# Attention scores without the mask products: maximum and exponential over the seen columns only, in four pieces of 64 rows

## The reference

```python
# 16 heads, q and k of 128 + 64 features, 256 tokens, CHUNK = 64, Q_BLOCK = 128
q_chunk = (bi * Q_BLOCK + arange(Q_BLOCK)) // CHUNK      # bi = 0, 1
key_chunk = arange(256) // CHUNK
mask = key_chunk[None, :] <= q_chunk[:, None]            # a chunk sees itself and those before it
sc = einsum('bqhd,bkhd->bhqk', qb, k) * 192 ** -0.5
p = softmax(where(mask, sc, -inf))
out = einsum('bhqk,bkhd->bqhd', p, v)
```

## Time and profile before

| | |
|---|---|
| median of 3 runs | 1943.89 us (1943.64 to 1944.12) |
| the profiled execution, its own time | 1943.84 us |
| its span in the trace | 1942.4 us |
| PE busy | 1936.6 us, 100% of the span |
| PE weight loads (PEld) | 1649.1 us, 85% |
| DVE busy | 1336.7 us, 69% |
| ACT busy | 1000.7 us, 52% |
| latent attention's heads (first scores to last gate) | about 174 to 284 us |

### The profile page before, as it was taken

One profiled execution on the slowest core, in us unless ns is written; L12 is line 12 of the kernel. 1 busy time (PEld: TensorE's weight loads), 2 busy tenths in 40 slices (PEclk: granted clock), 3 DMA queues, 4 the chain that ended last, 5 costly groups with the idle time before them and its releaser, 6 DMA issues.

```text
span 1942.4 us, 25506 instructions
## 1 busy us (share of the span) xinstructions
PE 1936.6 (100%) x10030; PEld 1649.1 (85%) x10030; DVE 1336.7 (69%) x1963; ACT 1000.7 (52%) x1433; POOL 0.2 (0%) x4
## 2 busy tenths in 40 slices
PE   9999999999999999999999999999999999999999
PEld 7889988988888888898888888888888888888887
DVE  6756778887545557898688877589666444666654
ACT  5645555675556544575565655444444334444442
POOL 0000000000000000000000000000000000000000
PEclk9999999999999999999999999999999999999999
DMA  8555325455553455545534345555555555555562
GB/s 328 176 193 174 131 90 192 174 199 187 191 189 133 174 192 195 182 177 207 211 116 149 128 152 195 196 194 177 191 195 200 197 201 192 190 189 194 185 228 109
DMA packets 51707, 353.23 MB, mean 182 GB/s; under 512 B 5652, under 2 KB 7196, under 8 KB 9860
## 3 DMA queue, kind: packets, MB, share of 16 engines
q1 hardware_dynamic: 50016, 348.84, 50.2%
q10 hardware_dynamic: 1572, 2.75, 0.4%
HBM read 349.47 MB, written 2.11 MB: 181 GB/s over the span
## 4 chain that ended last, share of the span: by engine, by line
PE 93%; DVE 5%; ACT 1%; issue 1%; DMA 0%; ACTq 0%; DVEq 0%
PE bank L1197 92%; DVE WL L2121 2%; DVE AR L2298 0%; ACT WH L1624 0%; DVE ft L2882 0%; DVE AR L2411 0%; DVE XP L2294 0%; DVE AR L2408 0%; DVE XP L2396 0%; PE bank L1342 0%; DMA X<-in_x 0%; DVE AR L2287 0%; PE bank L1427 0%; DVE AR L2322 0%; DVE AR L2321 0%
## 5 line engine op out<-in xcount | busy, mean ns | idle before, releaser
L1624 ACT ACTIVATE WH<-raw 128x1024 fp32r<-128x1024 f32 x649 | 683.4, 1057 | 645.1 <-PE bank L1197 639.0
L2121 DVE TENSOR_TENSOR WL<-raw,WH 128x1024 fp32r<-128x1024 f32 x649 | 784.0, 1221 | 316.4 <-ACT WH L1624 313.1
L1197 PE MATMUL bank<-XP,WH 128*128 128x512 f32 (+2 forms) x1584 | 498.6, 389 | 0.6 <-DVE WL L2117 0.3
L1197 PE MATMUL bank<-WH,FP 128*128 128x512 f32 x1408 | 434.7, 389 | 0.1
L1197 PEld LDWEIGHTS bank<-XP,WL 128*128 128x128 f32 x1504 | 281.8, 187 | 59.4 <-issue 0.7
L1197 PEld LDWEIGHTS bank<-WH,FP 128*128 128x128 f32 x1408 | 264.3, 188 | 56.1 <-DVE WL L2121 1.0
L1197 PE MATMUL bank<-XP,WL 128*128 128x256 f32 (+1 forms) x1504 | 308.5, 279 | 0.1
L1197 PE MATMUL bank<-WH,XP 128*128 128x512 f32 (+1 forms) x960 | 301.2, 389 | 0.3 <-DVE WL L2121 0.3
L1197 PE MATMUL bank<-WL,FP 128*128 128x512 f32 x704 | 273.9, 389 | 0.0
L1197 PEld LDWEIGHTS bank<-XP,WH 128*128 128x128 f32 (+1 forms) x1584 | 248.1, 187 | 7.5 <-issue 1.4
L1197 PE MATMUL bank<-WH,AP 128*128 128x512 f32 x704 | 217.2, 389 | 0.0
(11 more groups left out here) (336 smaller groups left out, 1616.9 us busy)
## 6 DMA issues: line engine op xcount, KB each, us to landing
raw<-in_W SPq DMA_DIRECT2D x326, 1024.0 KB, 4.8
out<-XT ACTq DMA_DIRECT2D x8, 256.0 KB, 2.0
raw<-in_W SPq DMA_DIRECT2D x3, 512.0 KB, 6.7
X<-in_x SPq DMA_DIRECT2D x3, 512.0 KB, 12.6
AR<-rv SPq DMA_DIRECT2D x1, 1024.0 KB, 5.9
cst<-in_cst SPq DMA_DIRECT2D x1, 899.5 KB, 11.7
raw<-in_W SPq DMA_DIRECT2D x2, 256.0 KB, 4.3
AR<-in_sgu SPq DMA_DIRECT2D x1, 512.0 KB, 5.7
```

The lines of the kernel that those rows point to most:

```text
L1197: return pe.matmul(o, lhsT, rhs, start=start, stop=stop)
L1624: ac.activation(w_slot(WH, s), raw_half(hf), ACT.Copy).then_inc(s_hi, 1)
L2121: tt(w_slot(WL, s), raw_half(pl.half_of[s]), w_slot(WH, s).bitcast(F32), ALU.subtract).then_inc(s_lo, 1)
```

## The change

The two mask products of each head go, and `uv` with them. `max` and `exp` no longer run over all rows at once, one instruction for each query block, but in four pieces of 64 rows, each over the columns that these rows see: 64, 128, 192 and 256 columns. The columns that rows 0 to 63 don't see are set to zero once, in all four buffers `Pm`, ahead of the section; `exp` never writes them, and `norm`, `turn` and `pv` run over them as before. The constants `u` and `v` become unused room.

```diff
-        uv = sb("uv", 256, BF, at=a0_ + 4 * 15616)
+        SEEN = [(j, slice(64 * r, 64 * r + 64), slice(128 * j, (128, 384)[j] - 64 + 64 * r))
+                for j in range(2) for r in range(2)]
...
                     for j in range(2):
-                        mm(S[:, 0:128], a[j][:, 0:128], k[j][:, 0:128], j == 0, False)
-                    mm(S[:, 0:128], uv[:, 0:128], uv[:, 128:256], False, True)
+                        mm(S[:, 0:128], a[j][:, 0:128], k[j][:, 0:128], j == 0, j == 1)
                     for j in range(2):
-                        mm(S[:, 128:384], a[j][:, 128:256], k[j], j == 0, False)
-                    mm(S[:, 256:384], uv[:, 0:128], uv[:, 128:256], False, True).then_inc(s_msc, 1)
+                        ins = mm(S[:, 128:384], a[j][:, 128:256], k[j], j == 0, j == 1)
+                    ins.then_inc(s_msc, 1)
...
-                    ac.activation(p[:, 0:128], S[:, 0:128], ACT.Exp, scale=sc, bias=m[:, 0:1], accum_out=s[:, 0:1])
-                    ac.activation(p[:, 128:384], S[:, 128:384], ACT.Exp, scale=sc, bias=m[:, 1:2],
-                                  accum_out=s[:, 1:2]).then_inc(s_mex, 1)
+                    for j, rows, cols in SEEN:
+                        ins = ac.activation(p[rows, cols], S[rows, cols], ACT.Exp, scale=sc, bias=m[rows, j:j + 1],
+                                            accum_out=s[rows, j:j + 1])
+                    ins.then_inc(s_mex, 1)
...
-                    dv.tensor_copy(uv[:, 0:128], C("u"))
-                    dv.tensor_copy(uv[:, 128:256], C("v")).then_inc(s_krm, 1)
+                    for p in Pm:
+                        for o in (64, 320):
+                            ins = dv.memset(p[0:64, o:o + 64], 0.0)
+                    ins.then_inc(s_krm, 1)
...
-                    dv.tensor_reduce(m[:, 0:1], S[:, 0:128], AX, ALU.max)
-                    chain(dv.tensor_reduce(m[:, 1:2], S[:, 128:384], AX, ALU.max))
+                    for j, rows, cols in SEEN:
+                        ins = dv.tensor_reduce(m[rows, j:j + 1], S[rows, cols], AX, ALU.max)
+                    chain(ins)
                     ts(m, m, -sc, None, ALU.mult).then_inc(s_mmx, 1)
```

More of the change, by code:

```diff
@@ L142 @@
 for _name, _w in [("ident", 128), ("bones", 128), ("U", 128), ("mC", 256), ("mS", 384), ("tril", 128),
-                  ("R12", 256), ("u", 128), ("v", 128), ("invf", 1), ("rowv", 1), ("ones", 128),
+                  ("R12", 256), ("room", 256), ("invf", 1), ("rowv", 1), ("ones", 128),
                   ("eps", 5)]:
@@ L184, in constants @@
     put("R12", r12)
-    put("u", (i < 64)[None, :])
-    put("v", np.where(i >= 64, NEG, 0.0)[None, :])
     f = (np.float64(10000.0) ** (-np.arange(0, 64, 2, dtype=np.float64) / 64)).astype(np.float32)
```

## The result

The changed kernel takes 1948.53 us, median of 16 runs (1946.72 to 1948.94), beside 1943.87 for the kernel before (16 runs, 1943.45 to 1944.20): 4.66 us more, 0.24% by the medians. The forecast was 1945.4 with a range up to 1947.5. The sign was right, the size was not.

A forecast was written before the change was run, and what follows sets the result against it. The prediction took the kernel to be bound by PE (93% of the chain). Its terms, -2.2 + 0.44 + 0.86 + 2.46 = +1.6 us, entered as 1943.89 + 1.5 = 1945.4 us, range 1941.2 to 1947.5.

The forecast's parts named there:

- What PE saves: On PE, dropping both mask products saves 0.22 us a head, 3.5 us over 16 heads.
- What the pieces cost: Without overlap, a maximum on DVE gets 0.68 us longer; exp on ACT releases its bank 1.05 us later.
- the overlap rival: Pieces overlap as whole instructions do: maximum +0.41, exp +0.68 us, kernel at 1943.1; chance 0.20.
- Heads 3, 7 and 10: Scores there wait for the exp two heads earlier: stalls of 0.44, 0.86 and 0.28 us.
- The other early heads: Over a microsecond, or several, lies between exp and scores there, so no stall was counted.
- The memsets and the low halves: Zeroing ahead of the section makes DVE's low halves up to 1.4 us late once, hidden by 16 tiles of cover.
- the forecast's list of early ones: Hand-overs from exp to the scores two heads on, with slacks of 0.61, 0.19 and 0.77 us at heads 3, 7, 10.
- The tail: From the last values on, late maxima and exps make PE 2.46 us late by `pv` 12, swallowing its mask savings there.
- 2.0 late: DVE's lateness from gate 6 to gate 10: 1.54 plus four maxima (2.7 us) against 2.3 us of waits for PE.
- exp 14's 1.17: Exp 14 takes 1.17 us longer on ACT ahead of gate 10's high part, making DVE's lateness about 2.46.
- All hidden: Rival: slack hides all longer maxima and exps, PE keeps 3.5 us, kernel at 1940.4; chance 0.10.
- The loop of DVE and ACT: Rival: six late heads each pay maximum plus exp, 1.85 us; +7.4 us in all, 1951; chance 0.09.

The follow-up runs named there:

- order experiment: Changed kernel with its four pieces reordered: both pieces of rows 0 to 63 first, then both of rows 64 to 127; 1945.63 us.
- the masks alone: Changed kernel, still without mask products, but with maximum and exponential whole again as in the kernel before; 1941.17 us.
- filler run: Changed kernel with three products of constants, read by nobody, put on PE ahead of head 12's scores; 1946.99 us.
- masks kept: Kernel before with both mask products left in, and maximum and exponential both in four pieces; 1950.22 us.
- the bare wait: Kernel before with four useless ACT copies of constants ahead of exp of head 10, nothing of the change in it; 1946.81 us.

## Why the prediction was wrong

**What PE saves: right.** Matmul by matmul the gain is 0.22 a head. The Trainium skill's figure (TensorE: Matmul & The Clock Gate, Back-to-back issue gap), by which the estimate was 0.16 a head, is too low here; the traces have 0.11 for each of these products.

**What the pieces cost: right.** 1.95 from the start of an exp to its release, three reductions ahead of the last in 0.89 us, both as worked out for the pieces themselves. The order experiment shows that what holds them is the change of start row, which the forecast took from the earlier trace rows. So the overlap rival falls: the overlap that it priced comes back with two gaps of three on the same rows, and the kernel is then 1.8 us faster among the runs at clock 1.000 (1946.87 to 1945.08) and 2.3 among the others.

**Heads 3, 7 and 10: right** within 0.04 us each. The other early heads' scores wait for no exp, as said. The memsets and the low halves cost nothing, as said: nothing moved between 23 and 173 us, and no low half stands in the waits from 160 to 300.

**Ahead of the last values: missed 0.4 us.** The weight load waits 0.31 there for DVE's copy of the last head's key, a hand-over that the forecast's list of early ones, all from exp to scores, did not have. Pieces of the maximum alone lose 0.37 from 226 to 243 us, half of it here, the masks alone 0.02, pieces of exp alone nothing: it is DVE, which has longer maxima while PE comes sooner. The forecast looked for DVE's lateness in the tail alone.

**The tail is the step that failed.** It said "Exp 10 starts at 256.93 and releases at 258.88; head 12's scores start at 258.93 in place of 256.95", and gave that wait the price of idle time. The wait came, at 2.75 us on the weight loads. But PE without a product for 2.5 us came out of it at 1.2 GHz, and the scores of head 12 and the weight products behind them ran 1.6 us longer (1.7 between the medians of the two heaps). The filler run shows that the idle stretch is what it takes: with products in it, ten runs of ten keep the full clock. The profile of before had no such stretch to read: its longest wait in this section is 0.5, and nothing in the forecast asked what PE does after a long one.

The smaller part of the miss is the size of the tail's terms. The forecast's term for the tail was 2.46 (how it follows from "2.0 late" and exp 14's 1.17 is not written out there); by the matmuls the tail lost 3.2 us without the clock and 4.7 with it. Head 12 loses 2.53 rather than 2.14, as exp 10 starts 1.37 late against PE's place at the last values, not 0.94. The two traces show nearly all of these 0.43. The gate product starts 0.82 later behind the longer maximum, forecast 0.68: the pieces take 0.70 more, and the product starts 0.20 behind the small TENSOR_SCALAR, 0.08 before. The other two parts are ACT's. Timeline of ACT in the changed kernel:

```profile
248.72 1.09 ACT L1708 ACTIVATE AR<-bank 128x512 f32<-128x512 f32 x2
249.83 0.42 ACT L1733 ACTIVATE XP<-AR 128x256 fp32r<-128x256 f32 x1
...
255.89 1.04 ACT L1622 ACTIVATE WH<-raw 128x1024 fp32r<-128x1024 f32 x1
256.95 0.49 ACT L1730 ACTIVATE AR<-bank 128x384 f32<-128x384 f32 x1
```

These instructions of all 128 rows start 1.11 and 1.06 apart and no longer overlap; in the kernel before it was 0.97 and 0.95, and with the maximum alone in pieces it still is, while pieces of exp alone give 1.11 and 1.06. So exp in pieces also takes the overlap from whole instructions some way behind it, 0.14 and 0.11 here, which the forecast had at nothing. Behind head 12 the net is +0.78, forecast +0.48. The whole difference of 3.2 us is 0.5 at the start, 0.4 ahead of the last values, 0.1 of small steps, 0.4 at head 12, 0.3 behind it and 1.6 of clock, less 0.1 at heads 3, 7 and 10.

**The rivals.** All hidden is out: PE waits 6.7 us. The loop of DVE and ACT is out too, although its side of the result came nearer than its price: the tail does lose more than 2.46, but at three places (head 12, `pv` 11, `pv` 12) and by the clock, not 1.85 at each of six heads.

The forecast gave 0.10 to a kernel slower by over 0.2%, and it came out slower by 0.24%, just beyond that line. The range was too narrow above for a reason that could be named beforehand: it let the waits vary, and not the speed of PE behind them. Without the fall of the clock the kernel takes 1946.9, inside it.

**What stays open.** In which runs the clock falls: 13 of 16 in the changed kernel, 5 of 10 with rows first, 5 of 7 with masks kept, 2 of 10 with the bare wait, at gaps of 2.2 to 2.6 us between products, each gap read in the one profiled execution of its kernel. The gap's length does not order them: the bare wait has the longest and the fewest falls. That it depends on what PE did before the gap or on where the gap falls would fit, but no run here separates them. The fall itself stands in the windows of the changed kernel alone; the profiled executions of the other three kernels are of their lower heaps, and of their other runs only the mean clock of 0.999 is known. Nor is it shown where the step in the first 20 us comes from, or why the parts of the waits at `pv` 11 and `pv` 12 split as they do between DVE and ACT.

## What to carry to other kernels

Before an instruction is cut into row blocks, price the pieces as queued one behind the other, and order them so that the start row changes as rarely as possible: that alone was worth 1.8 us here between runs at the full clock and 2.3 between the others. Work taken from PE counts only up to the next hand-over; list the slack at each hand-over for each engine that gets longer, the copies behind the longer instruction included. And when a change opens a gap in PE like this one (2.2 to 2.6 us here) in a kernel that had none, put the price of its next products at half clock into the range, or cover the gap with any product at hand.

## What the runs showed of the hardware

TensorE's clock fell from 2.4 to 1.2 GHz for 3.4 us in the trace of the changed kernel, at the end of a gap of 2.5 us. Four kernels with gaps of 2.2 to 2.6 us have some runs with a mean clock of 0.999 and others of the same kernel with 1.000, 1.1 to 2.0 us apart between the medians of the two heaps; that the place is the same in the other three is not shown. There was no such run among the 61 of the six kernels with a gap of 1.3 us or less ahead of head 12, nor in the ten with the filler. ACT, too, holds an ACTIVATE that starts on other rows than the one before it: behind a 64x64 piece the next starts after 0.40, or after 0.29 on the same rows; behind one of 64x128 after 0.47 or 0.36. Whole instructions behind an exp in pieces lost 0.14 and 0.11 us of their overlap. And 2 us of products that nobody uses made the changed kernel 1.5 us faster.
